# Lead-in of a two-block kernel: vector c by columns, copies on two engines, scale sums first, a product repeated in waits

## The reference

```
mod = silu(c) @ mod_w + mod_b            # c: 1024, mod_w: 1024 x 3072
shift, scale, gate = split(mod, 3)
h = rmsnorm(x, norm_g) * (1 + scale) + shift
u = h @ w_in                             # then gated convolutions, a linear recurrence, w_out
...
x = x + (1 + gate) * y;  rmsnorm(x, final_g)
```

## Time and profile before

| | us |
|---|---|
| median of 3 runs | 2136.63 |
| lowest, highest | 2135.2, 2137.69 |
| profiled execution | 2136.5 |
| its span on the core | 2134.7 |
| mean granted TensorE clock | 0.97 |

### The profile page before, as it was taken

How to read it: one execution, slowest core, us unless ns; L and a number is a source line. 1 busy time by engine, 2 the same in 40 slices (tenths; PEclk the granted TensorE clock), 3 DMA queues, 4 the chain that set the end, 5 groups by cost and what they waited for, 6 DMA issues and landing times.

```text
span 2134.7 us, 23884 instructions
## 1 busy us (share of the span) xinstructions
PE 2031.3 (95%) x9072; PEld 1667.7 (78%) x9072; DVE 1270.9 (60%) x1370; ACT 803.6 (38%) x1010; POOL 966.0 (45%) x540
## 2 busy tenths in 40 slices
PE   4999999999999999999998998988999999999997
PEld 3788788887788888878886877766888888788874
DVE  7789998878542476546402785488655555613137
ACT  4342356565442313221232344445444333402132
POOL 1375745555222222233311116557877788722262
PEclk7999999999999999999997999998999999999998
DMA  9641112122112332548654955241222222153132
GB/s 374 196 151 34 48 49 72 55 72 72 40 60 79 119 109 70 172 120 308 218 165 131 313 181 163 84 148 60 60 60 60 89 80 79 60 197 127 36 101 101
DMA packets 268670, 251.40 MB, mean 118 GB/s; under 512 B 8258, under 2 KB 230211, under 8 KB 268563
## 3 DMA queue, kind: packets, MB, share of 16 engines
q1 hardware_dynamic: 265475, 238.42, 35.4%
q10 hardware_dynamic: 3088, 11.54, 1.4%
HBM read 206.08 MB, written 43.84 MB: 117 GB/s over the span
## 4 chain that ended last, share of the span: by engine, by line
PE 49%; issue 14%; DVE 5%; POOL 3%; DMA 1%; ACT 1%; SPq 1%; ACTq 0%; POOLq 0%; DVEq 0%
PE PS L2109 17%; PE PS L1657 15%; PE PS L2001 5%; PE PS L1896 5%; POOL wl L815 2%; PE PS L2123 2%; DVE B L2888 1%; PE PS L1954 1%; PE PS L1819 1%; PE PS L1947 1%; PE PS L1948 1%; PE PS L2035 1%; PE PS L1909 1%; DVE B L2887 1%; DMA SCR<-um_d 0%
## 5 line engine op out<-in xcount | busy, mean ns | idle before, releaser
L815 POOL TENSOR_TENSOR wl<-raw,wh 128x1024 fp32r<-128x1024 f32 (+1 forms) x157 | 378.4, 2411 | 824.9 <-ACT wh L1044 602.6
L1657 PE MATMUL PS<-XH,wh 128*128 128x512 f32 x1424 | 443.5, 393 | 8.3 <-POOL wl L815 2.8
L1657 PE MATMUL PS<-XH,wl 128*128 128x512 f32 x1424 | 441.2, 391 | 0.0
L1657 PE MATMUL PS<-XL,wh 128*128 128x512 f32 x1424 | 440.5, 391 | 0.0
L1657 PEld LDWEIGHTS PS<-XH,wh 128*128 128x128 f32 x1424 | 268.0, 189 | 67.5 <-issue 4.5
L1657 PEld LDWEIGHTS PS<-XH,wl 128*128 128x128 f32 x1424 | 269.3, 189 | 56.4
L1657 PEld LDWEIGHTS PS<-XL,wh 128*128 128x128 f32 x1424 | 268.9, 189 | 56.2
L1044 ACT ACTIVATE wh<-raw 128x1024 fp32r<-128x1024 f32 (+1 forms) x108 | 111.0, 1028 | 440.2 <-PE PS L1657 187.5
L2321 DVE SCALAR_TENSOR_TENSOR PS<-B,PJ,PS 128x1022 f32<-128x1022 f32 (+7 forms) x197 | 251.1, 1275 | 7.5
L1114 ACT ACTIVATE wh<-raw 128x1024 fp32r<-128x1024 f32 x48 | 50.8, 1058 | 263.8 <-PE PS L1657 248.8
L975 POOL TENSOR_TENSOR wl<-SCR,wh 128x512 fp32r<-128x512 f32 x80 | 114.1, 1428 | 70.5 <-ACT wh L1496 70.5
(11 more groups left out here) (412 smaller groups left out, 3750.4 us busy)
## 6 DMA issues: line engine op xcount, KB each, us to landing
B<-in_ada_w SPq DMA_DIRECT2D x48, 512.0 KB, 5.3
raw<-in_ffn_up_w SPq DMA_DIRECT2D x48, 512.0 KB, 4.3
raw<-in_w_in SPq DMA_DIRECT2D x40, 512.0 KB, 4.9
raw<-in_m_in_w SPq DMA_DIRECT2D x37, 512.0 KB, 5.0
mod_tiles<-in_mod_w SPq DMA_DIRECT2D x16, 512.0 KB, 13.0
raw<-in_w_out SPq DMA_DIRECT2D x16, 512.0 KB, 4.8
qkvo_d<-B SPq DMA_DIRECT2D x16, 512.0 KB, 3.5
raw<-in_m_out_w SPq DMA_DIRECT2D x16, 512.0 KB, 4.1
```

Of the source, the lines that this page charges most:

```text
L815: tt(wl[slot][:, 0:kc, :], raw[slot][:, 0:kc, :], wh[slot][:, 0:kc, :].bitcast(F32), ALU.subtract).then_inc(lo_done, 1)
L1657: last = mm(ps[:, c:c + step_n], W[:, k, :], Y[:, k, c:c + step_n], start=(seen == 0), stop=(seen == total - 1))
```

## The change

- **SP** gets one DMA ahead of the stage rows: c straight from DRAM into SC[:, 4, :], one element at a time with channels on partitions (1,024 pieces of four bytes). c also stays among the staged rows.
- **ScalarE**, behind its DMA issues: waits for c, makes Silu(c) into column 0 of CA, then copies the odd blocks of the transposed x (1, 3, 5, 7) out of PS[1], and only then starts the ten squares. Three Silus remain behind PV.
- **VectorE** copies only the even blocks. Then mod_sum(0), which waits for the first Silu; then PV, the diagonal and mod_sum(1). PV and the diagonal stood ahead of mod_sum(0) before.
- **TensorE** waits for the copy of the right engine in its transposes; before the add-ups it now waits for the copies of the context's transposes (ctxT_sb), and behind the first add-up it multiplies avg with PV five times (128x128 by 128x512, into PS[0], result unused), behind the second eight times.
- Waits for all copies become two waits, one for each engine.

```diff
+            with nc.allow_non_contiguous_dma(reason="one small vector by columns"):
+                sp.dma_start(SC[:, 4, :], A["c"][0].rearrange("(k p) -> p k", p=P)).then_inc(ev("c_in"), 16)
             sp.wait_ge(*at("stage_zero", 1))
...
             act.wait_ge(*at("consts", 3))
+            act.wait_ge(*at("c_in", 16))
+            f(CA[:, :, 0], SC[:, 4, :], ACT.Silu).then_inc(ev("ca"), 1)
+            for c in range(1, NT, 2):
+                act.wait_ge(*at("xT_ps", c + 1))
+                f(B2[:, :, c * P:(c + 1) * P], PS[1][:].rearrange("p (k t) -> p k t", k=KD), ACT.Copy).then_inc(ev("xT_act"), 1)
             for c in range(NT + NC):
...
-            for n, name in enumerate(("c", "c", "c_2", "c_ctx")):
+            for n, name in ((1, "c"), (2, "c_2"), (3, "c_ctx")):
...
                 if c >= 2:
-                    pe.wait_ge(*at("xT_sb", c - 1))
+                    pe.wait_ge(*at("xT_act" if c % 2 else "xT_sb", c // 2))
...
             pe.wait_ge(*at("pv", 1))
-            for q, (acc, c0) in enumerate(((T[4], KD), (T[0], 0))):
+            pe.wait_ge(*at("ctxT_sb", 1))
+
+            def keep_busy(n):
+                for _ in range(n):
+                    mm(PS[0][:, 0:512], avg[:], PV[:, 0:512], start=True, stop=True)
+
+            for q, (acc, c0, idle) in enumerate(((T[4], KD, 5), (T[0], 0, 8))):
                 pe.wait_ge(*at("mod_sum", q + 1))
                 for c in range(KD):
                     last = mm(MOD_PS[:, c0 + c:c0 + c + 1], acc[:, c * P:(c + 1) * P], ones[:], start=True, stop=True)
                 last.then_inc(ev("mod_sum_used"), 1)
+                keep_busy(idle)
...
-            for c in range(NT):
+            for c in range(0, NT, 2):
                 dve.wait_ge(*at("xT_ps", c + 1))
                 V.tensor_copy(B2[:, :, c * P:(c + 1) * P], PS[c % 2][:].rearrange("p (k t) -> p k t", k=KD)).then_inc(ev("xT_sb"), 1)
-            dve.wait_ge(*at("stage_ps", 1))
-            V.tensor_copy(PV[:], PS[2][:, 0:NST * P]).then_inc(ev("pv"), 1)
-
-            dve.wait_ge(*at("rms", 1))
             dve.wait_ge(*at("consts", 3))
...
-            diagonals(T[3], NT + NC, "diag")
...
-            dve.wait_ge(*at("ca", 4))
-            for q in range(2):
-                mod_sum(q)
+            dve.wait_ge(*at("ca", 1))
+            mod_sum(0)
+            dve.wait_ge(*at("stage_ps", 1))
+            V.tensor_copy(PV[:], PS[2][:, 0:NST * P]).then_inc(ev("pv"), 1)
+            dve.wait_ge(*at("rms", 1))
+            diagonals(T[3], NT + NC, "diag")
+            mod_sum(1)
```

More of the change, by code:

```diff
@@ L113, in block_pair_kernel @@
         share("pe_stage", *((n, 1) for n in ("stage_ps", "r_ps", "ctxT_ps", "mean_ps", "var_ps", "ln_r", "stat1_ps", "n1_r2", "n1_r1", *(f"{n}{h}" for h in range(2) for n in ("n2_ps", "n3_ps")), "n4_ps0", "n4_ps1")))
-        share("act_stage", *((n, 1) for n in ("rms", "lam_e", "ctxn", "ln_sd", "n1_sd1", "n1_sd2", "f_e", "n2_sd0", "n3_sd0", "n2_sd1", "n3_sd1", "n4_sd0", "n4_sd1")))
+        share("act_stage", ("xT_act", NT // 2), *((n, 1) for n in ("rms", "lam_e", "ctxn", "ln_sd", "n1_sd1", "n1_sd2", "f_e", "n2_sd0", "n3_sd0", "n2_sd1", "n3_sd1", "n4_sd0", "n4_sd1")))
         for a, b, n in (("xsh", "w_ok", KD), ("xsl", "va_ok", KD), ("i_ok", "kw_ok", KD), ("r_ok", "t_ps", KD), ("th_ok", "e_ok", KD),
                         ("m2", "q2_ok", KD), ("mult_ok", "d_ok", KD), ("lx_sb", "s_ps", KD), ("ls_sb", "den_ps", KD), ("a_ok", "num_ps", KD),
-                        ("xT_sb", "hs_ok", NT)):
+                        ("xT_sb", "hs_ok", NT // 2)):
             share(f"{a}_then_{b}", (a, n), (b, 0))
@@ L131, in block_pair_kernel @@
             share(f"{a}_then_{b}", (a, n), (b, 0))
+        share("c_in_then_lf_out", ("c_in", 16), ("lf_out", 0))
         share("pool_stage", ("msum_zero", 1), ("pads_zero", 1))
@@ L528, in _ @@
                 sp.wait_ge(*at(f"mod_in{q}", 32))
-            sp.wait_ge(*at("xT_sb", NT))
+            sp.wait_ge(*at("xT_sb", NT // 2))
+            sp.wait_ge(*at("xT_act", NT // 2))
             sp.dma_start(xT_d.rearrange("(k p) t -> p k t", p=P), B2[:]).then_inc(ev("xT_out"), 16)
@@ L1749, in _ @@
             pe.wait_ge(*at("ctxn", 1))
-            pe.wait_ge(*at("xT_sb", NT))
+            pe.wait_ge(*at("xT_sb", NT // 2))
+            pe.wait_ge(*at("xT_act", NT // 2))
             for c in range(NC):
@@ L2255, in _ @@
             dve.wait_ge(*at("ctxT_ps", 1))
+            dve.wait_ge(*at("xT_act", NT // 2))
             for k in range(KD):
@@ L2370, in _ @@
             dve.wait_ge(*at("xl_L1", KD))
+            dve.wait_ge(*at("ca", 4))
             gate_sum()
```

## The result

| | before | after |
|---|---|---|
| median, us | 2135.91 (4 runs) | 2151.45 (4 runs) |
| lowest to highest | 2132.34 to 2137.69 | 2150.25 to 2153.52 |
| profiled execution | 2136.5 | 2150.82 |
| its span, mean granted clock | 2134.7, 0.97 | 2149.0, 0.971 |

The change makes the kernel slower, by 0.7%: ratio 1.0072, interval 1.0059 to 1.0085. The profiled executions differ by 14.3 us, the medians by 15.5; the prediction was 2149.7, a shift of 13.2 us.

What follows compares the result with a forecast made beforehand. TensorE, busy 95%, was taken as the bound, its start set by the second add-up's end: root 42.2 + 17.7 = 59.9 against 46.74, shift +13.2. 2136.5 + 13.2 = 2149.7 us; range 2139 to 2156.

Steps and rivals of the forecast that it cites:

- c's DMA: SP's queue: c's pieces alternate with x's packets, landing at 17.3 us; issue delay of 0.4 us costs nothing.
- The first rival: DMA queues: c lands early, near 9 us, several pieces per turn; +3.1, 2139.7 us; chance 0.18.
- ScalarE's order: ScalarE's queue: odd copies ahead of all ten squares put the root at 42.2 us, 20.8 later than before.
- Rival 4: ScalarE's queue: the copies' order matters, c hardly; c near 13 us, shift of 6 to 9; chance 0.10.
- rival 1: DMA queues: c lands early, root at 31.9 to 32.3, second add-up at 49.6 to 50.0; 2139.7 us; chance 0.18.
- The scale sum first: VectorE: first sum ends at 37.8 within the root's wait; costs nothing, brings nothing where the root is late.
- The two misjudged terms: TensorE between context copies and second add-up: first add-up 1.84 us at full clock, five repeats 4.4 to 4.7.
- rival 2: TensorE's add-ups and five repeats: clock drops in the gap before the first add-up; 2154 to 2158 us; chance 0.12.
- The eight repeats: TensorE behind the second add-up: 7.1 us, full-clock opening, gain lost waiting for unit 2; worth 0, price 0.
- Behind unit 2: Rest of the kernel after unit 2 starts: nothing edited, so the forecast added no term there.
- The bound of 3.8 us on any gain: Lead-in: at most 2.0 us from an earlier second sum plus 1.74 from its add-up at full clock.

Runs made afterwards that it cites:

- e7: Kernel before plus only the DMA of c by columns at the head of SP's queue, its result unused: 2140.06 us, ratio 1.0020.
- e8: Kernel before with the odd copies on ScalarE ahead of its ten squares, nothing else of the change: 2150.43 us, ratio 1.0066.
- e1: Changed kernel with c's DMA on ScalarE's queue ahead of x: 2141.14 us, ratio 1.0017.
- e2: Changed kernel with ScalarE's wait for c and its Silu behind the four odd copies: 2144.95 us, ratio 1.0033.
- e5: Changed kernel without the five repeats between the add-ups; the eight and the wait stay: 2145.94 us, ratio 1.0038.
- e6: Changed kernel without the eight repeats behind the second add-up; the five stay: 2150.47 us, ratio 1.0066.
- e12: Kernel before with three and four repeats behind the add-ups, PJ's wait moved, GpSimd's low parts behind the second sum: 2133.11 us, ratio 0.9988.
- e13: e12 without its repeats and TensorE's wait for the context's copies: 2135.63 us, ratio 0.9993.
- e10: Kernel before with three and four repeats behind the add-ups and ScalarE's wait for PJ moved to first need: 2136.30 us, ratio 0.9998.
- e9: Kernel before with each odd copy on ScalarE behind the square of its own block: 2143.88 us, ratio 1.0033.
- e4: Changed kernel without its thirteen repeats and without TensorE's wait for the context's copies: 2147.18 us, ratio 1.0048.
- e11: e9 with GpSimd waiting for the second sum before its low parts: 2139.43 us, ratio 1.0018.

## Why the prediction was right

The steps in their order:

| step | predicted, us | measured, us |
|---|---|---|
| c lands | 17.3 | 16.9 |
| last odd copy ends | 28.7 | 27.6 |
| root | 42.2 | 40.9 |
| first sum, PV | 37.8, 38.8 | 36.7, 37.6 |
| second sum ends | 53.9 | 52.5 |
| context's copies end | 51.7 | 50.9 |
| first add-up | 1.84 | 3.55 |
| five repeats | 4.4 to 4.7 | 6.23 |
| second add-up ends | 59.9 | 62.4 |
| opening starts | 67.0 | 68.8 |
| unit 2 | 90.9 | 93.2 |
| shift of the profiled execution | +13.2 | +14.3 |

**c's DMA.** Right, and for the reason given: turn and turn about, one packet for one. The first rival (c early) fell by the 95 to 95 packets, and the Trainium skill's account of whole groups of descriptors ("DMA: Bandwidth & Descriptors", "Queues, rings and completion order") is not what this trace shows for these two queues. The even counts in windows of 0.2 us speak against it, not the landing: groups of one size in both queues would have landed c just as late. The statement that the DMA costs SP's queue nothing was wrong in itself (e7: +4 us) and harmless here.

**ScalarE's order.** Right. The root was taken 1.3 us too late: c was 0.4 us early, and blocks 3 to 7 were transposed a little faster than I had them. e8 shows that the order alone, without c, moves the root to 31.6; c's lateness adds the other 9.3 us. Rival 4 (c hardly matters) falls with e1 and e2. e1 is also rival 1's case: its root was out at 32.5 (31.9 to 32.3 by the rival), but the second add-up ended at 54.20 and not at 49.6 to 50.0, by the terms misjudged below.

**The scale sum first.** "Brings nothing where the root is late" is wrong, though the sum of the prediction had the effect in it. What brought nothing was the early end of the first sum as such: it was ready at 36.7 and lay until 51.1. But with the first sum done inside the wait for the root, only the diagonal and the second sum stood behind the root. From the root to the end of the second sum it took 11.6 us in after (40.88 to 52.50) and in e1 (32.52 to 44.15), against 21.8 in before (21.34 to 43.11) and 25.8 in e8, which has the old order (31.62 to 57.44, 4.0 of them beside GpSimd). The edit kept some 10 us off the loss. No run changes this order alone; the figures are read from these four timelines.

**The two misjudged terms.** Behind 2.1 idle us, the first add-up and half of the five repeats ran at 1.2 GHz. I had taken full clock, because it "had held through 4.2 us idle before". That window ends at 33.20. Before's own first add-up begins 0.14 us later, behind that same gap, and it ran at 1.2 GHz (TensorE's timeline of before, and its window with the granted clock, 0.50):

```profile
33.34 3.55 PE L1760 MATMUL PS<-ones,SCR 128*128 128x1 f32 x16 [4.42 <-DVE SCR L2235]
```

```profile
33.40:36.90 3.50, 3.49 (x16) 0.50 1.04 409
```

So the row was no evidence that the clock is full behind a gap, and the step was wrong already on the trace of before. What happened is rival 2's mechanism at half its price: 9.5 us from the start of the first add-up to the start of the second, against 6.4 in the forecast and 12.7 in the dearest case of the rival. It makes +3.1 against the -0.6 by which the first add-up began earlier. From the root to the end of the second add-up the forecast had 17.7 us, after took 21.5 and e1 21.7. Five traces have this gap of 2.12 us: in four of them (after, e1, e2, e5) the add-up ran mostly or wholly at 1.2 GHz, in e6 at full clock. So this term changes from trace to trace, and a forecast should have carried it as a choice between two values.

**The eight repeats.** Right: the opening ran at full clock from its first record, TensorE then waited 2.00 us for unit 2's low weights (2.5 predicted, 1.29 before), and e6 shows no price and no gain in the lead-in.

**Behind unit 2.** "Nothing is edited" held for the program, but not for the time: unit 2 is 15.5 us late, the profiled execution 14.3. In the low-clock spell at 171 us, which was shorter than in before, 1.6 us came back; some 0.5 were lost again later, which was not traced. So the lead-in was 2.3 us dearer than the forecast's 13.2, and a gift of 1.2 that no step named brought the total near. That 14.3 is so close to 13.2 is partly luck.

**The bound of 3.8 us on any gain.** Not tested by this change, and e12's 3.6 us in the lead-in only look like it. The bound was 2.0 for an earlier second sum and 1.74 for the add-up. In e12 the sum ended at 43.16, no earlier than before; 1.6 us are the add-up at full clock, and the other 2.0 lie between it and unit 2, where unit 2's high weights waited for TensorE (70.36) and no longer for the table PJ. The bound had no such term.

## What to carry to other kernels

Before a small load is put at the head of a queue, count its pieces and what runs in the other queue: each piece waits one turn of that queue, and so does all that stands behind it. An in-order engine that is handed copies ahead of its own chain should get each copy behind the chain's step for the same block, since otherwise the chain inherits every wait of the copies. Work that does not need the late result belongs ahead of the wait for it: here that was worth some 10 us. A repeated product that keeps the clock up has to be over when the awaited operand comes; behind it in the queue it costs its full length, at the clock that happens to hold.

## What the runs showed of the hardware that was not expected

**Gapless one-column products at a low clock.** In e5, 32 such records ran from 51.0 to 58.0 with 6.99 of 7.00 us busy and the clock stayed at 0.50; it rose to 1.00 about 3 us into the 512-column repeats behind them. In before the clock fell within the one-column sums, with TensorE busy all the time: 1.00 from 154.0 to 155.7, 0.57 from 155.7 to 159.3. The 32 records behind the earlier trace rows took 6.53 us in before, 4.44 in after, 3.72 in e12. From unit 2's start to the next such group (at 185.99 in before) it took 108.3 us in before and e13, 106.7 in after and 105.1 in e12; all fourteen traces show one of these three values. So the time can differ by up to 3.3 us with a stretch in which all kernels do the same work, as much as several of the effects in this document.

**VectorE and GpSimd hold each other up.** Seven sum steps took 9.21 us alone and 11.17 (e8), 11.37 (e10) and 13.13 us (e9) beside GpSimd's two low-part instructions, which took 4.64 us alone and 5.63 to 6.45 beside them; a VectorE step of 0.17 us lasted until GpSimd's ended (e4; in before, too, it took 0.66 us and ended at 47.64, GpSimd's pair at 47.61). With GpSimd made to wait (e11) both were as fast as alone. The Trainium skill, "SBUF — State Buffer", "SBUF: two separate sides", has the two share one pair of ports, held by one instruction as a whole when VectorE reads two operands from SBUF; e4's two ends, 56.94 and 56.97, agree with that.

**Four-byte packets.** 95 of them took 5.5% of 16 engine microseconds, 9 ns each, but the 1,024 of c delayed the rows behind them by 4 us and more (staged vectors at 22.2 instead of 18.2).
